# Modulation tiles in fours and a narrow block at each end of the first stage

## The reference

```
mod   = silu(c) @ ada_w + ada_b            # ada_w: 2048 x 6144, float32
shift, scale, gate = split(mod, 3)         # the same with c_ctx for the context
h     = rms_norm(x, norm_w) * (1 + scale) + shift
q, k, v, z = split(h @ w_in, 4)            # w_in: 2048 x 8192
```

## Time and profile before

| | us |
|---|---|
| median of 3 runs (2076.32 to 2077.63) | 2076.57 |
| the profiled execution | 2077.76 |
| its span, first to last instruction | 2075.9 |
| PE busy (97% of the span) | 2017.7 |
| first piece starts | 49.03 |
| last piece ends | 152.12 |
| head 1's probabilities start to be turned | 199.13 |

### The profile page before, as it was taken

The page is one execution under the profiler, slowest core; times in us unless marked ns, Lnnn a source line. Parts: engine busy times, 40 slices in busy tenths (PEclk is TensorE's granted clock), DMA queues, the critical chain, the costliest instruction groups (busy, mean ns, idle before and its releaser), DMA issues.

```text
span 2075.9 us, 31012 instructions
## 1 busy us (share of the span) xinstructions
PE 2017.7 (97%) x10458; PEld 1674.5 (81%) x10458; DVE 1459.5 (70%) x2076; ACT 967.6 (47%) x1398; POOL 665.7 (32%) x568
## 2 busy tenths in 40 slices
PE   5998999999999999999999999999999999999998
PEld 3567888888888888878878888888888888888886
DVE  5248777777777777774348877787878787777544
ACT  3244444455444544453355445445444544456443
POOL 1035666556565655635200111111112111110011
PEclk7999999999999999999999999999999999999999
DMA  9996667666666666656353554554554645556654
GB/s 352 338 261 140 168 177 184 174 173 168 172 174 178 178 171 173 164 141 172 102 152 98 149 147 125 144 147 125 143 149 114 167 116 147 138 148 199 226 184 153
DMA packets 422706, 349.23 MB, mean 168 GB/s; under 512 B 13600, under 2 KB 366464, under 8 KB 422016
## 3 DMA queue, kind: packets, MB, share of 16 engines
q1 hardware_dynamic: 397552, 273.43, 46.0%
q0 software_dynamic: 19968, 70.26, 14.1%
q10 hardware_dynamic: 5136, 4.89, 0.7%
HBM read 344.21 MB, written 4.33 MB: 168 GB/s over the span
## 4 chain that ended last, share of the span: by engine, by line
PE 82%; DVE 7%; DMA 4%; ACT 3%; issue 3%; POOL 1%; SPq 0%; DVEq 0%; POOLq 0%; ACTq 0%
PE bank L373 21%; PE bank L377 20%; PE bank L375 20%; DMA arena<-in_na_ada_w_dram 3%; PE bank L2303 3%; PE bank L2305 2%; PE bank L2304 2%; DVE w_lo L357 2%; PE bank L2241 1%; DVE arena L1647 1%; PE bank L2222 1%; PE bank L2107 1%; PE bank L1995 1%; PE bank L2022 1%; PE bank L2236 1%
## 5 line engine op out<-in xcount | busy, mean ns | idle before, releaser
L373 PE MATMUL bank<-act_hi,w_hi 128*128 128x512 f32 (+1 forms) x2448 | 906.0, 370 | 11.5 <-DVE w_lo L357 7.0
L377 PE MATMUL bank<-act_hi,w_lo 128*128 128x512 f32 (+1 forms) x2448 | 888.6, 363 | 0.0
L375 PE MATMUL bank<-act_lo,w_hi 128*128 128x512 f32 (+1 forms) x2448 | 888.0, 363 | 0.0
L357 DVE TENSOR_TENSOR w_lo<-arena,w_hi 128x2048 fp32r<-128x2048 f32 x184 | 435.2, 2365 | 210.8 <-ACT w_hi L353 147.9
L373 PEld LDWEIGHTS bank<-act_hi,w_hi 128*128 128x128 f32 x2448 | 462.7, 189 | 97.3 <-issue 14.4
L377 PEld LDWEIGHTS bank<-act_hi,w_lo 128*128 128x128 f32 x2448 | 462.5, 189 | 73.6
L375 PEld LDWEIGHTS bank<-act_lo,w_hi 128*128 128x128 f32 x2448 | 463.2, 189 | 68.8
L620 POOL TENSOR_TENSOR acc<-acc,arena 128x512 f32<-128x512 f32 x224 | 328.5, 1467 | 126.5 <-ACT arena L858 117.2
L353 ACT ACTIVATE w_hi<-arena 128x2048 fp32r<-128x2048 f32 x138 | 263.8, 1911 | 84.5 <-PE bank L2305 78.2
L1415 DVE SCALAR_TENSOR_TENSOR arena<-arena,cond_c 128x512 f32<-128x512 f32 x240 | 249.4, 1039 | 63.9 <-DMA arena<-in_ssd_ada_w_dram 37.6
L858 ACT ACTIVATE arena<-arena,cond_c 128x512 f32<-128x512 f32 x256 | 171.3, 720 | 261.1 <-POOL acc L620 151.0
(11 more groups left out here) (253 smaller groups left out, 2157.8 us busy)
## 6 DMA issues: line engine op xcount, KB each, us to landing
arena<-in_ssd_w_in_dram SPq DMA_DIRECT2D x81, 1024.0 KB, 6.0
arena<-in_na_w_in_dram SPq DMA_DIRECT2D x58, 1024.0 KB, 7.3
arena<-in_ssd_ada_w_dram POOLq DMA_DIRECT2D x96, 512.0 KB, 4.1
arena<-in_na_ada_w_dram SPq DMA_DIRECT2D x64, 512.0 KB, 8.0
arena<-in_ssd_w_out_dram SPq DMA_DIRECT2D x32, 1024.0 KB, 5.1
arena<-in_na_ada_w_dram POOLq DMA_DIRECT2D x32, 512.0 KB, 4.2
arena<-in_na_w_out_dram SPq DMA_DIRECT2D x16, 1024.0 KB, 6.3
arena<-cs_scr SPq DMA_DIRECT2D x64, 256.0 KB, 5.5
```

Source lines behind the costliest of these rows:

```text
L357: nc.vector.tensor_tensor(w_lo[:, n0 % 2, :], raw[slot], w_hi[:, n0 % 2, :].bitcast(F32), ALU.subtract).then_inc(s_lo, 1)
L373: nc.tensor.matmul(out[:, 0:cols], hi[:, w], act_hi3[:, k, 0:cols], start=(k == 0), stop=False)
L375: nc.tensor.matmul(out[:, 0:cols], hi[:, w], act_lo3[:, k, 0:cols], start=False, stop=False)
L377: mm = nc.tensor.matmul(out[:, 0:cols], lo[:, w], act_hi3[:, k, 0:cols], start=False, stop=(k == KT - 1))
```

## The change

The blocks become (0,2), (2,4), (6,4), (10,4), (14,2): one narrow block at either end, three wide ones between. There are still 32 tiles, 24 wide and 8 narrow, and the same bytes. The weight sets move along (`AHEAD`, `BEHIND`). PE takes the tiles of the wide blocks 2 and 3 in fours: four pieces, four tiles, three pieces, four tiles, then the columns and one piece. In block 1 it takes two tiles, one piece and six tiles. Block 4's four tiles come in a row behind six pieces. `norm_rows` stands behind two tiles instead of three. GpSimd issues the first two loads of the gate's sums behind its last two context halves instead of ahead of them. In the first heads ScalarE's part 3 comes ahead of the turned probabilities, and VectorE's part 2 ahead of the split of tile 7 and part 3 ahead of the probabilities' low parts; two of GpSimd's loads swap places with steps of the bias.

```diff
...
@@ -49,11 +50,11 @@
 PRE = 6
 PRE_BANK = (4, 5, 6, 7, 0, 1)
 PRE_AT = (0, 2, 4, 5, 1, 3)
-BLOCKS = ((0, 4), (4, 4), (8, 4), (12, 2), (14, 2))
+BLOCKS = ((0, 2), (2, 4), (6, 4), (10, 4), (14, 2))
 FIRST_K = [k0 for k0, _ in BLOCKS]
-ADA_USED = [2 * k0 if nk == 4 else 24 + 2 * (k0 - 12) for k0, nk in BLOCKS] + [32]
-AHEAD = (0, 2, 4, 6, None)
-BEHIND = (1, 3, 5, None, 7)
+ADA_USED = list(itertools.accumulate([0] + [2 * nk for _, nk in BLOCKS]))
+AHEAD = (0, 1, 3, 5, None)
+BEHIND = (None, 2, 4, 6, 7)
 N_OUT_A = 4 * HEADS
 N_DT = N_OUT_A + KT
 N_SSD = N_DT + 1
@@ -622,9 +623,6 @@
             for k in range(KT):
                 if k in FIRST_K:
                     pool.wait_ge(s_mod, FIRST_K.index(k) + 1)
-                if k == KT - 2:
-                    load_ada(0, None, True)
-                    load_ada(1, None, True)
                 if k >= 3:
                     pool.wait_ge(s_h, k - 2)
                 nc.gpsimd.tensor_scalar(hx[k % 3][:, LAT:TOK], xn_t[:, k, LAT:TOK], gain_a[:, 1, k:k + 1],
@@ -648,6 +646,8 @@
                 nc.gpsimd.tensor_tensor(bias, bias, mask[:, :].unsqueeze(1).broadcast_to([P, 6, GRID_W]),
                                         ALU.add).then_inc(s_bias, 1)
 
+            load_ada(0, None, True)
+            load_ada(1, None, True)
             pool.wait_ge(s_h, KT)
             load_bias(None)
             add_products(0, None)
@@ -656,11 +656,11 @@
             add_products(1, None)
             load_ada(3, None, True)
             add_products(2, None)
+            load_ada(4, None, True)
             load_bias(1)
-            load_ada(4, None, True)
             add_products(3, None)
+            load_ada(5, None, True)
             mask_bias(1)
-            load_ada(5, None, True)
             for l in range(4, 7):
                 add_products(l, None)
                 if l + 2 < 8:
@@ -921,11 +921,12 @@
                 nc.scalar.activation(k_hi, bank[1][:, :], ACT.Copy).then_inc(s_khi_k, 1)
                 products(2, Turn())
                 exp_scores(Turn())
+                products(3, Turn())
                 turned_probs(Turn())
                 act.wait_ge(s_used, 7)
                 nc.scalar.activation(v_t, bank[2][:, :], ACT.Copy).then_inc(s_free[0], 1)
                 next_hi(4, Turn(base=4))
-                for l in range(3, 8):
+                for l in range(4, 8):
                     products(l, Turn())
 
             first_heads()
@@ -1500,13 +1501,14 @@
                 query_low(bank[0], Turn(base=1))
                 key_low(bank[1], Turn(base=1))
                 softmax(none)
+                ada_part(2, none)
                 split_lo(dve, 7, none, 1)
                 normalise(none)
                 v_low(none)
-                ada_part(2, none)
+                ada_part(3, none)
                 probs_low(none)
                 split_lo(dve, 8, none, 0)
-                for l in range(3, 6):
+                for l in range(4, 6):
                     ada_part(l, none)
                 gate_o(none, backwards_free(o_t[:, 0, :]))
                 for l in range(6, 8):
@@ -2028,42 +2030,39 @@
                 if p % 4 == 3 and k < KT - 1:
                     mm.then_inc(s_kused, 1)
 
-            for q in range(8):
-                mod_products(0, q)
-                if q == 2:
-                    norm_rows()
+            mod_products(0, 0)
+            mod_products(0, 1)
+            norm_rows()
+            mod_products(0, 2)
+            mod_products(0, 3)
             mod_columns(0)
-            for c in (1, 2):
-                for q in (0, 2, 4, 6):
-                    if q < 6:
-                        first_tiles(c - 1, q)
-                        first_tiles(c - 1, q + 1)
+            first_tiles(0, 0)
+            first_tiles(0, 1)
+            mod_products(1, 0)
+            mod_products(1, 1)
+            first_tiles(0, 2)
+            for q in range(2, 8):
+                mod_products(1, q)
+            mod_columns(1)
+            first_tiles(0, 3)
+            for c in (2, 3):
+                for p in range(4):
+                    first_tiles(c - 1, p)
+                for q in range(4):
                     mod_products(c, q)
-                    mod_products(c, q + 1)
-                first_tiles(c - 1, 6)
+                for p in range(4, 7):
+                    first_tiles(c - 1, p)
+                for q in range(4, 8):
+                    mod_products(c, q)
                 mod_columns(c)
                 first_tiles(c - 1, 7)
-            for q in range(2):
-                first_tiles(2, 2 * q)
-                first_tiles(2, 2 * q + 1)
-            mod_products(3, 0)
-            mod_products(3, 1)
-            for p in range(4, 6):
-                first_tiles(2, p)
-            mod_products(3, 2)
-            mod_products(3, 3)
-            first_tiles(2, 6)
-            mod_columns(3)
-            first_tiles(2, 7)
-            mod_products(4, 0)
-            mod_products(4, 1)
-            first_tiles(3, 0)
-            mod_products(4, 2)
-            mod_products(4, 3)
-            first_tiles(3, 1)
+            for p in range(6):
+                first_tiles(3, p)
+            for q in range(4):
+                mod_products(4, q)
+            first_tiles(3, 6)
             mod_columns(4)
-            for p in range(2, 4):
-                first_tiles(3, p)
+            first_tiles(3, 7)
             for p in range(4):
                 first_tiles(4, p)
             pe.sem_inc(s_used, PRE)
```

More of the change, by code:

```diff
@@ L15 @@
+import itertools
 from contextlib import ExitStack, contextmanager
```

## The result

The changed kernel takes 2092.44 us (median of four runs, 2090.29 to 2095.25) against 2077.1 before (median of four): slower by more than the spread, ratio 1.0072, 95% interval 1.0059 to 1.0084. The forecast was 2077.8, no change, with a range to 2087.5. The profiled execution after has a span of 2089.9 us, 14.0 more than before.

What follows compares the result with a forecast made beforehand. DMA and PE were both taken as nearly the bound in wide blocks, tied through four slots. Stage 8 us later minus 6.8 gained in the first heads gives +1.2 us: 2077.8 against the median, no change; range 2071 to 2087.5.

Steps and rivals of the forecast that it cites:

- Steps 1 and 2: Start and block 1: first piece at 40.4 instead of 49.03; last tile at 61.9, 9.5 us early.
- Step 3: Blocks 2 and 3, tiles in fours: 28.6 us per block instead of 27.1, losing 3.0 us together.
- a rival: First stage: the clock falls in the new tile waits; 2081.2 us with one fall, 2087 with three; chance 0.22.
- no single wait there is as long as the 2.69 us: Argument against falling clock in the wide blocks, comparing their waits with PE's earlier 2.69 us for low weights.
- Step 4: End of the first stage: it ends at 159.1 instead of 152.12, 7.0 us later; taken as 8.
- the 0.8 us for GpSimd's two loads: End of stage: 0.8 us go because GpSimd no longer issues two loads ahead of its context halves.
- The check by PE's own work: First stage: counting PE's pieces, four more tiles and 14 us more waits, less 8.6, gives 9 us later.
- Step 5: First heads: earlier gate's sums remove the 5.54 us wait and half clock; gain 7.8 us, 6.8 after giving back 1.0.
- That split was done 3 to 4 us ahead of need, so nothing: First heads: VectorE's part 2 ahead of the split of tile 7 costs 1.5 us there, but nothing overall.
- The giving back behind head 1: First heads: 1.0 us given back for waits in heads 2 and 3, PE being 1.3 us further ahead.

Runs made afterwards that it cites:

- e3: The changed kernel plus matmuls whose result nobody reads in PE's waits for tiles of blocks 1 to 3; 2085.34 us, ratio 1.0034 to the kernel before.
- e2: The changed kernel's first stage with the gate's sums placed as before; 2097.42 us, ratio 1.009 to the kernel before.
- e1: The kernel before with only the early gate's sums of the change, first stage as before; 2074.55 us, ratio 0.9982 to the kernel before.
- e6: e1 with VectorE's part 2 back behind the low values; 2074.14 us, ratio 0.9985 to the kernel before.
- e4: The changed kernel with blocks 2 and 3 back in twos, one piece ahead of the columns; 2088.91 us, ratio 1.0048 to the kernel before.
- e5: The changed kernel with the first four tiles of blocks 2 and 3 behind two pieces instead of four; 2083.09 us, ratio 1.0025 to the kernel before.
- e10: e4 with block 1's first four tiles before block 0's columns, block 4's behind four pieces, part 2 back, unread matmuls early; 2072.37 us, ratio 0.9976.

## Why the prediction was wrong

**Steps 1 and 2, right.** First piece 40.4 forecast, 40.81 measured; block 1's last tile 61.9, measured 62.57. The dry queue in 43 to 50 us was as worked out (3 GB/s in 44 to 48).

**Step 3, wrong in its sum: this is the step that failed.** "The sum is 28.6 us" was worked out with every instruction at full clock, and so put the half clock at nothing. e3, at full clock, measures 29.5 and 29.4, so the chain was right and 0.8 to 0.9 short; the real blocks take 32.5 and 33.4. The forecast left the clock to a rival and gave it 0.22. The price of one fall stood there nearly right, 3.4 us where the first cost 3.0; for blocks 2 and 3 it had "up to 3 us each", and the second fall cost 4.1. There were two falls, at 57 to 71 and at 95 to 105 us. The argument "no single wait there is as long as the 2.69 us" was worth nothing. Before the falls the waits are 0.72, 1.61 and 1.63 us, and 1.12 and 1.68, with a tile of 1 us between them. The row that should have decided was the one that I quoted for the rival, block 0 at half clock with PE busy for 1.94 of every 2.71 us. Block 3, with nearly the same waits of 1.38 and 1.65, kept the full clock, and in e2 it fell with 1.22 and 1.64; from the traces I can't say beforehand which of two such stretches falls. The section "HAM oscillation" of the Trainium skill's page "TensorE: Matmul & The Clock Gate" says that short bursts of matmuls with DMA waits between them run slow one after the other. Its example has waits of 3 to 5 us; here waits of 0.7 to 1.7 did it, in two of three blocks, and in all three of e2.

**Step 4, right.** e1 bears out the 0.8 us for GpSimd's two loads: its wait for the last low weights is 1.85 instead of 2.69. From block 3's last tile to the last columns 23.5 forecast, 23.8 measured; from the columns to the last set's pieces 6.6 and 6.6; the last four pieces 9.9 and 9.9. The check by PE's own work gave 9 us; it assumed the same clock and so could not see the fault.

**The stage.** Worked out 7.0, taken 8, measured 16.65. The 9.65 us that the working lacks are, within 0.1, 7.1 for the clock in blocks 2 and 3 (3.0 and 4.1), 1.6 for its 0.8 per block, 0.7 for block 1, and 0.3 behind. The forecast's 8 took 1 us of that as a reserve.

**Step 5, right in its mechanism, too high in size.** Forecast 6.8, measured 4.15 (16.65 - 12.50). The chain of the sums moved as forecast and the long wait went but for 0.70. (The working's own terms, 5.54, 2.0 and 0.4, add up to 7.9 and not to the 7.8 that it carries on.) "That split was done 3 to 4 us ahead of need, so nothing" is the part that failed: part 2 took 1.95 us, and the probabilities' scaling behind it 3.06 for two instructions that take 0.88 elsewhere, since it now runs beside a GpSimd addition (180.35; in e1 it is the same, and in e6, without an addition beside it, 0.88). What mattered was not the split's slack but that of the scaling behind it, 1.9 us. The giving back behind head 1 was 1.3 (2.08 against the 0.80 of before) where I had 1.0. Not all of the 4.15 belongs to the sums: e2, with the sums as before, also gets 0.75 us back behind its late stage (20.64 to 19.89).

**Behind head 4.** 12.50 us at head 4 are 14.0 at the end. PE's waits there are the same in both to 0.3 us, but layer 1's start loses more to the clock. The windows of before and after:

```profile
1080.00:1100.00 20.00, 17.05 (x68) 13.78 (x67) 20.00 (x43) 14.73 (x31) 0.00 (x0) 0.83 0.46 129
```

```profile
1080.00:1100.00 20.00, 15.32 (x69) 12.54 (x69) 13.20 (x23) 13.25 (x24) 0.46 (x2) 0.79 0.86 247
1100.00:1120.00 20.00, 20.00 (x85) 16.44 (x85) 17.95 (x36) 9.52 (x22) 0.79 (x2) 0.95 0.11 26
```

A mean clock of 0.83 over 20 us is (1 - 0.83) / 0.5 times 20, or 6.8 us at half clock; 0.79 and 0.95 are 8.4 and 2.0, together 10.4. At half clock PE does half the work, so 3.6 us more of it cost up to 1.8 us. That covers the 1.5, but no run isolates it. The forecast had no term for it, and nothing in the change touches this place. It is not the changed kernel's alone: from 1060 to 1140 us the granted clock is 0.94 in it, e2, e4 and e5, and 0.96 in before and the others.

Forecast +1.2 us, measured +14.0 in the profiled spans: 8.65 in the stage beyond the 8 taken, 2.65 in the first heads, 1.5 behind them: 12.8, the difference. The largest single part, 7.1 us, was missed in the mechanism: the sum had no term for the clock.

## What to carry to other kernels

Where transfers go through a few slots, look at how late the first slot of a group comes free, not at how many are freed at once: e5's fours cost nothing, the same fours two pieces later about 2.3 us a block, and more through the clock. A stretch in which PE is fed tile by tile has to be priced at half clock in the sum itself, with everything behind it up to the next long run of matmuls. Half clock costs nothing where the transfers set the pace anyway (e10 up to block 2) and nearly all of it where PE is behind them (e3). A PE that arrives earlier waits longer, and can lose its clock in that very wait (e10).

## What the hardware showed that was not expected

- Waits of 1.1 and 1.7 us with 1 us of matmuls between them brought the clock from 1.0 to 0.5 in block 2; 1.4 and 1.65 did not in block 3, and 1.2 and 1.6 did in block 3 of e2, which has the same stage.
- Matmuls that nobody reads, 50 of them beside the real ones in e3, made the changed kernel 7 us faster (2092.44 to 2085.34), 6.4 of it in the first stage.
- A VectorE scaling pair of 0.88 us took 3.06 beside a GpSimd addition (in the changed kernel and in e1).
